# One prompt of a hybrid decoder layer with expert retrieval: all tokens in one stream, or two token streams with the second one's work placed between the expert slots

## The reference

```
h  = rmsnorm(x) @ w_in                       # columns split among four mixers
x += rmsnorm_g(mixers(h)) @ w_out            # RWKV-7, FoX attention, gated unit, dilated attention
x += cross_attend(rmsnorm(x), memory)        # 4 heads over 256 memory tokens: ca_wq, ca_wk, ca_wv, ca_wo
x += peer(rmsnorm(x))                        # expert retrieval
y  = rmsnorm(x)

def peer(x):                                 # 8 heads, 128 x 128 experts, 16 kept per head
    q = x @ peer_wq
    s = q . peer_keys                        # two halves of 128 keys per head
    e, score = the 16 best sums of both halves
    act = gelu(x . u_tab[e])                 # u_tab, v_tab: 16384 rows of 1024
    return sum(softmax(score) * act * v_tab[e])
```

## Time and profile before

| | |
|---|---|
| median of 3 runs | 1295.68 us (1295.6 to 1297.0) |
| the profiled execution | 1299.01 us, span of the trace 1297.2 us |
| mean granted clock of PE | 0.948 |
| PE, DVE, ACT, POOL busy | 1100.2, 658.9, 446.5, 380.4 us |
| first fetch of expert rows issued | 542.99 us |
| moved by all DMA queues | 387.99 MB |

### The profile page before, as it was taken

One profiled execution on the slowest core, in us unless ns is written; L12 is line 12 of the kernel. 1 busy time (PEld: TensorE's weight loads), 2 busy tenths in 40 slices (PEclk: granted clock), 3 DMA queues, 4 the chain that ended last, 5 costly groups with the idle time before them and its releaser, 6 DMA issues.

```text
span 1297.2 us, 12851 instructions
## 1 busy us (share of the span) xinstructions
PE 1100.2 (85%) x4406; PEld 604.8 (47%) x4406; DVE 658.9 (51%) x1685; ACT 446.5 (34%) x1249; POOL 380.4 (29%) x382
## 2 busy tenths in 40 slices
PE   5999999796888997989999987788777877877776
PEld 4777877564566765644444432232222322322211
DVE  2361222455311222456576666767666666667554
ACT  3232210333202212144443444434544344444343
POOL 0410012550000000124444455344443443434430
PEclk9999996897988998989999999999999999999989
DMA  9431131842164863489999999999999999999995
GB/s 306 131 99 33 33 118 58 285 150 78 45 244 153 353 242 98 141 329 416 387 428 415 401 410 427 427 427 426 426 426 427 427 426 427 426 427 427 426 427 213
DMA packets 96642, 387.99 MB, mean 299 GB/s; under 512 B 8320, under 2 KB 53312, under 8 KB 57152
## 3 DMA queue, kind: packets, MB, share of 16 engines
q0 software_dynamic: 43520, 306.24, 56.9%
q1 hardware_dynamic: 50752, 78.83, 17.5%
q10 hardware_dynamic: 2304, 2.10, 0.5%
HBM read 381.19 MB, written 5.42 MB: 298 GB/s over the span
## 4 chain that ended last, share of the span: by engine, by line
PE 53%; DMA 29%; ACT 9%; DVE 5%; POOL 2%; issue 2%; ACTq 0%; SPq 0%; POOLq 0%; DVEq 0%
DMA near<-peer_uv,idx 19%; PE ps L1106 15%; PE ps L606 14%; PE ps L614 9%; DMA far<-peer_uv,idx 8%; PE ps L714 1%; ACT L1389 1%; ACT L1400 1%; ACT dg L1409 1%; DVE near L1953 1%; PE ps L1088 1%; ACT wv L1404 1%; PE ps L985 1%; PE ps L610 1%; PE ps L1026 1%
## 5 line engine op out<-in xcount | busy, mean ns | idle before, releaser
L1106 PE MATMUL ps<-near,dg 128*128 128x512 f32 (+1 forms) x852 | 419.2, 622 | 80.2 <-ACT dg L1409 80.2
L2043 POOL DMA_INDIRECT near<-peer_uv,idx x213 | 232.6, 1092 | 404.5 <-PE ps L1106 286.0
L1953 DVE CUSTOM_DVE_ANT_0 near<-near,XN 128x1024 f32<-128x1024 f32 x192 | 235.3, 1225 | 154.3 <-DMA near<-peer_uv,idx 153.9
L1106 PEld LDWEIGHTS ps<-near,dg 128*128 128x128 f32 (+1 forms) x852 | 149.9, 187 | 313.3 <-ACT dg L1409 179.6
L1106 PE MATMUL ps<-far,dg 128*128 128x512 f32 (+1 forms) x300 | 148.7, 625 | 44.3 <-ACT dg L1409 44.3
L606 PE MATMUL ps<-xT,W 128*128 128x288 f32 x672 | 182.8, 416 | 1.3 <-DVE xT L1452 0.9
L1400 ACT ACTIVATE gl<-act 128x1 f32<-128x1 f32 x288 | 57.9, 201 | 326.0 <-DVE act L1953 325.7
L606 PEld LDWEIGHTS ps<-xT,W 128*128 128x128 f32 x672 | 129.5, 195 | 64.1 <-issue 34.6
L1409 ACT ACTIVATE dg<-const,wv 128x128 f32<-128x128 f32 (+1 forms) x288 | 113.0, 393 | 19.3 <-PE ps L1106 10.3
L1106 PEld LDWEIGHTS ps<-far,dg 128*128 128x128 f32 (+1 forms) x300 | 48.8, 179 | 142.9 <-ACT dg L1409 98.0
L2043 POOL DMA_INDIRECT far<-peer_uv,idx x75 | 78.7, 1049 | 109.8 <-PE ps L1106 101.7
(11 more groups left out here) (393 smaller groups left out, 1131.3 us busy)
## 6 DMA issues: line engine op xcount, KB each, us to landing
W<-w_in SPq DMA_DIRECT2D x11, 1024.0 KB, 5.5
MR<-mk_s SPq DMA_DIRECT2D x8, 1024.0 KB, 14.0
MR<-mv_s SPq DMA_DIRECT2D x8, 1024.0 KB, 10.6
W<-peer_wq SPq DMA_DIRECT2D x8, 1024.0 KB, 5.5
W<-ca_wk SPq DMA_DIRECT2D x4, 1024.0 KB, 5.7
W<-ca_wv SPq DMA_DIRECT2D x4, 1024.0 KB, 5.6
W<-w_out SPq DMA_DIRECT2D x4, 1024.0 KB, 6.6
W<-ca_wq SPq DMA_DIRECT2D x4, 1024.0 KB, 5.3
```

Of the source, the lines that this page charges most:

```text
L1106: ins = mm(PS[0:m, 2 + 2 * t + half, :], dg[:, n % DGS, 0:m], row(n)[:, D + half * 512:D + (half + 1) * 512], start=False, stop=False, ski ...
L1953: V.tensor_tensor_reduce(out=u, in0=u, in1=x, scale=1.0, scalar=0.0, op0=ALU.mult, op1=ALU.add, accum_out=M["act"][:, par, k:k + 1]).then_ ...
L2043: G.indirect_dma_start(row(n), None, io["peer_uv"], bass.IndirectOffsetOnAxis(ap=M["idx3"][:, it % 3, k:k + 1], axis=0))\
```

## The change

The tokens are split in two streams. Stream A has the 32 sample tokens and prompt rows 0 to 127 (160 columns), stream B prompt rows 128 to 255 (128 columns). The list `FIRST` takes A through all stages up to the key scores of heads 0 to 3 and the first selection; the fetches begin there. The list `THEN` holds the rest of A's scores and then all stages of B. It has 90 cuts, and 58 pairs of slots (`EARLY`) are spread over them evenly by `pairs_at`; the other 86 pairs follow behind the list. All of SP, PE, ACT and DVE follow the same two lists, so that a pair stands at the same cut on each. The weights of `w_in`, `w_out`, `ca_wq`, `ca_wo` and `peer_wq` are loaded twice, 72 blocks in all (32 of them for B); B's blocks use two of the three places, the third becomes a ring place (`w2`). The ring has five places, six from slot 10 and thirteen from slot 124.

A slot is now a group of 32 tokens, four heads, one rank: nine groups of 32 slots, 288 as before, 1 MB each. `dg` is 128x32, and PE combines a pair by four products of 32x512 in the four column groups of one bank (L1386). Behind a group ACT copies the bank out (`stash`; the first five go to HBM). `fin_load`, `fin_sum`, `fin_square`, `fin_scale` and `fin_store` put the groups together at set pairs. The token rows for the dots are loaded per group (`load_xr`, four broadcast copies); keys, memory keys and values and norm gains are loaded again for B, and the normed rows and the residual go through HBM. The waits of PE in a pair are for `act_dg` of the pair's second slot.

```diff
+BLOCKS = W_IN + MEMORY + TAIL + W_IN + TAIL
...
+        s = b % RING if b < SECOND else (b - SECOND) % 2
...
-NEAR, FAR = 8, 5
-WIDE = 6 * TOPK
...
+GROUPS = [0, 0, 0, 0, 2, 1, 1, 1, 1]
+NG = len(GROUPS)
+PER = 32
...
+NEAR, FAR = 5, 7
+WIDE = 124
...
-        + [("rounds", it) for it in range(NIT)] + [("finish", 2)])
...
+    THEN = (
+        [("lin", P_A + 4 + i) for i in range(4)] + [("score", ("A", 1)), ("first", 1), ("norm_b", None)]
+        + [("lin", IN_B + i) for i in range(4)]
+        + [("rw_pre", "B"), ("rw_kk", "B"), ("lin", IN_B + 4), ("rw_vec", "B"), ("rw_tile", 1), ("rw_scan", "B"),
+           ("rw_out", "B")]
+        + [("lin", IN_B + i) for i in range(5, 12)] + [("lf", "B")]
+        + [("attn", (1, s)) for s in range(11)]
+        + [("sgu", "B"), ("gnorm", ("B", (0, 2))), ("gnorm", ("B", (1, 3)))]
+        + [("lin", OUT_B + i) for i in range(4)] + [("norm", (0, "B"))] + [("lin", Q_B + i) for i in range(4)]
+        + [("cross", (1, s)) for s in range(7)]
+        + [("lin", O_B + i) for i in range(4)] + [("norm", (1, "B"))]
+        + [("lin", P_B + i) for i in range(4)] + [("score", ("B", 0))]
+        + [("lin", P_B + 4 + i) for i in range(4)] + [("score", ("B", 1))])
...
+    EARLY = 58
...
+        return range(c * EARLY // NCUTS, (c + 1) * EARLY // NCUTS)
...
+            for _ in range(n + 1):
+                for p in pairs_at(c):
+                    pair(p)
+                c += 1
+        assert c == NCUTS
+        for p in range(EARLY, PAIRS):
+            pair(p)
...
+            pe.wait_ge(*at("act_dg", n + 1))
...
-                    ins = mm(PS[0:m, 2 + 2 * t + half, :], dg[:, n % DGS, 0:m], row(n)[:, D + half * 512:D + (half + 1) * 512],
-                             start=False, stop=False, skip_group_check=True)
...
+            for x in (n, n + 1):
...
+                    rows = slice(64 * half + 32 * (x % 2), 64 * half + 32 * (x % 2) + 32)
+                    ins = mm(PS[rows, ACC, :], dg[:, x % DGS, :], row(x)[:, D + half * 512:D + (half + 1) * 512],
+                             start=x % PER < 2, stop=x % PER >= PER - 2, skip_group_check=True)
...
-                A(dg[:, n % DGS, 0:m], ident if t < 2 else cst("groupsum"), ACT.Copy, scale=M["wv"][:, par, col_k])\
...
+                A(dg[:, n % DGS, :], cst("groupsum"), ACT.Copy, scale=M["wv"][:, par, col_k]).then_inc(*inc("act_dg", n))
```

More of the change, by code:

```diff
@@ L136, in constants @@
     cols["groupsum"] = (r % TS == np.arange(TS)[None]) * 1.0
+    late = ("s_ab", "s_a", "batch", "lf_new_l", "lf_new_r", "sb_bias", "sd_bias")
+    cols = {k: cols[k] for k in [k for k in cols if k not in late] + list(late)}
     where, at = {}, 0
@@ L384, in program @@
     rT, kT, vT = hT[:, 0:2, :], hT[:, 2:4, :], hT[:, 4:6, :]
[L388 to L394, removed]
-        + [("rounds", it) for it in range(NIT)] + [("finish", 2)])
     X1, XN, gr, hX, QX, MK, MV, MR, SCx, PTx, SSx, PTy, softx = (
         M[k] for k in ("X1", "XN", "gr", "hX", "QX", "MK", "MV", "MR", "SCx", "PTx", "SSx", "PTy", "softx"))
[L398 to L425, removed]
+    keys, SA, dg, XR, FS, X1f, gF = (M[k] for k in ("keys", "SA", "dg", "XR", "FS", "X1f", "gF"))
     SC, PT, LFU, lf, soft = (M[k] for k in ("SC", "PT", "LFU", "lf", "soft"))
@@ new lines, in pair, with residual, add_group @@
+        def pair(p):
+            slot_pair()
+        def residual(t, name, count):
+            m = TILES[t][1]
+            pe.wait_ge(S.sem(name), 16 * count)
+            for half in range(2):
+                mm(PS[0:m, FIN_BANK[t] + half, :], ident[0:m, 0:m], X1f[0:m, SLOT[t], half * 512:(half + 1) * 512],
+                   start=True, stop=False, skip_group_check=True)
+        def add_group(t, j, place):
+            for half in range(2):
+                ins = mm(PS[32 * j:32 * j + 32, FIN_BANK[t] + half, :], cst("groupsum")[64 * half:64 * half + 64, :],
+                         FS[64 * half:64 * half + 64, place, :], start=False, stop=True, skip_group_check=True)
+            return ins
@@ L1951, in rounds, with pair @@
+        later = [iter(())]
+        def pair(p):
+            for n in (2 * p, 2 * p + 1):
+                it, k = divmod(n, TOPK)
+                g, par = n // PER, it % 2
+                if k == 0 and it:
+                    for _ in later[0]:
+                        pass
+                    later[0] = topk(it + 2) if it + 2 < NIT else iter(())
+                if n % PER == 0:
+                    dve.wait_ge(S.sem(f"xr{g % 2}_in"), 64 * (g // 2 + 1))
                 dve.wait_ge(S.sem(f"row{PLACE[n]}_in"), LANDINGS[n])
@@ L1971, in _ @@
             "rw_scan": rw_scan, "rw_sample": rw_sample, "rw_out": rw_out, "lf": log_forget, "attn": attn,
             "sgu": sgu, "sattn": sattn, "gnorm": gnorm, "norm": norm, "cross": cross, "scross_k": scross_k,
[L1973 to L1974 removed]
+            "scross_v": scross_v, "first": first, "fin_scale": fin_scale, "end": lambda: fin_scale(1)},
+            lambda label: None, pair)
     @block.gpsimd
```

1950 lines of the change are left out of this document (1143 added, 807 removed).

## The result

The changed kernel takes 1523.9 us (median of four, 1513.0 to 1534.0) against 1295.64 of the kernel before: a ratio of 1.177, 95% interval 1.167 to 1.187. The sign was forecast, the size was not: 1405 with a range to 1500. The profiled execution took 1518.75 us, its span is 1516.6.

The account below looks back on a forecast made before the run. First part bound by PE and waits between engines, second by bytes at 427 GB/s. 444 + 260 + 183 + 35 + 30 + 35 = 987, plus 408 + 13 + 10 = 1418, adjusted to 1405 us; range 1240 to 1500.

Parts of the forecast that it names:

- Part 2: Stream B by itself, its stages repeated at 128 columns without memory and sample work: 260 us, bounds 245 to 290.
- Part 5: Behind B: 166 slots at 2.456 are 408 us, other transfers 13, the end 10.
- (a): Rival: pairs in B hide behind other work, bytes stay the limit; 1227 us, range 1215 to 1293, chance 0.20.
- (b): Rival: pairs cost as forecast, but tables, clock and weights little; 1320 to 1340 us, slower, chance 0.12.
- (c): Rival: B's weight blocks land late behind fetches, 32 blocks add 200 us; 1580, beyond 1500 at chance 0.11.
- Part 1: Stream A with 160 columns starts fetches earlier: first fetch at 402 us instead of 543, B begins at 444.
- Part 3: 54 pairs within B: 21 behind weight blocks at 2.95 us, 33 elsewhere at 3.7, sum 183, bounds 48 to 217.
- Part 4: What mixing pairs into B adds: table loads 35 us, lower clock 30, waits for weights 35.

Follow-up runs that it names:

- all pairs in one place: Changed kernel with all 58 early pairs in one cut between the rest of stream A and B's first block, B without slots: 1516.7 us.
- three places: Changed kernel with three places instead of two for B's weights, and a ring of five instead of six until slot 124: 1484.2 us.
- pairs behind blocks: Changed kernel with B's 54 pairs only at cuts that follow a weight block, none at the other cuts: 1432.3 us.
- One pair later: Changed kernel with PE combining each pair at the place of the next pair, all else unchanged: 1406.5 us.

## Why the prediction was wrong

By its own parts, predicted and measured, in us:

| | predicted | measured | from |
|---|---|---|---|
| first fetch | 402 | 412 | the changed kernel |
| B begins | 444 | 454 | the changed kernel |
| B by itself (Part 2) | 260 (245 to 290) | 300 | all pairs in one place |
| 54 pairs and what they bring (Parts 3 and 4) | 183 + 35 + 30 + 35 = 283 | 600 - 300 = 300 | both |
| behind B (Part 5) | 408 + 13 + 10 = 431 | 462 | the changed kernel |
| sum | 1418 | 1516 | |

The mechanism was right: earlier fetches, a chain that stands in PE's stream, and the bytes behind it. Rivals (a) and (b) are out, the latter by 180 us. Of the 200 of (c) the run with three places found 40. The step that failed first of all is the price of a pair between units: 3.7 with an overlap that did not come, where the place above shows 5.65. Three other terms were too small as well, and so was the sum by the 10 that I took off for waits covering one another.

*Part 1* was late by 10, within its bounds of 385 to 415.

*Part 2* was 40 too small and 10 beyond its bound. In the run with all pairs in one place, read by stages, the products with weight blocks (and the two key scores) take 174 us where I counted 121; all else takes 126 where I counted 139. Of the 53 too many, 30.5 are PE's waits for blocks, with no pair in B; the longest:

```profile
PE ps L850 <- DMA W<-w_in: 12.0, 3, 6.7
PE ps L858 <- DMA W<-w_out: 8.5, 1, 8.5
```

My own figures had this. With two places a load goes out only when PE is done with the block that lay there, so two blocks take a landing and a block, 5.3 + 3.55 = 8.85, and not 7.1; over 32 blocks that is 28. That "at 5.3 nothing is late" needs the pairs between the blocks, and Part 2 is B without them.

A smaller part is the clock. I scaled the stages of the earlier trace rows by columns and tiles. But those rows hold stages in which PE's gaps were filled with products for the memory keys; B has no such filler. In the same run B's attention is at this clock, without any pair in it:

```profile
880.00:913.00 33.00, 27.74 (x80) 15.71 (x80) 14.75 (x49) 13.13 (x32) 0.00 (x0) 0.54 0.20 62
```

33 us at 0.54, where half of the 50 at 0.91 was expected. I had named that loss in Part 4's 30 for the clock, but sized it for B and the pairs together.

*Part 3.* The price between units was wrong in its choice: 3.7, between 4.7 for a serial chain and 2.7. In attention it is 5.65 (above), which is the serial chain with PE's part at the lower clock. The overlap that I allowed for is not there, because the dots stand behind the unit on DVE, and the unit's last step on DVE waits for PE. With the 4.7 of my upper bound, 33 pairs would have added another 33 us. PE's waits for `dg` were 210 us where I had named 100 to 150. With the 4.1 per pair of the run with pairs behind blocks, an estimate for the 33 others is (300 - 21 x 4.1)/33 = 6.5 each, table loads and clock included, where I had 3.7 + 1.2 = 4.9. These 1.6, some 53 us over 33 pairs, are what the pairs cost (300) above 183 + 35 + 30 = 248, my sum for them without the term for weights.

*Part 4*, term by term: table loads 35, measured 26. Weights 35: PE waits 29 for them in B, but 30.5 in B by itself, so the pairs added nothing to it; the number fits by luck, since I had put it down to landings behind fetches. Clock 30 (bounds 0 to 75): the zero products gave back 64, in B's own products and the pairs together. The first slot's 3.78 had shown the price at that level; I took it for an event at a stage's start. Here the 54 pairs keep PE busy for 91.7 us, 1.70 each, between the 1.06 and the 1.93 of the two levels, so most of them ran at the lower one.

The terms don't simply add. One pair later takes 117 off and three places 40; both together take 132. One later and pairs behind blocks take 117 and 92, and together 81.

*Part 5* was 31 too small. Behind B a slot does not take the 2.456 of the earlier trace rows. The DMA queues of 300 us, 1100 to 1400, in the changed kernel (all, the fetches, SP's loads), and the fetches of 900 to 1200 in the kernel before:

```profile
DMA packets 18480, 125.26 MB, mean 418 GB/s; under 512 B 2203, under 2 KB 2203, under 8 KB 3803
...
q0 software_dynamic: 16497, 120.13, 96.5%
q1 hardware_dynamic: 1825, 4.72, 4.5%
```

```profile
q0 software_dynamic: 17482, 127.30, 100.6%
```

120.13 MB are 114.6 slots in 300 us, 2.62 us each, against 121.4 and 2.47 before. From 1054 to the end the fetch queue moved 178.27 MB, 170 slots and not 166, since two slots beyond the 116 had landed by then and not six. 170 times 2.62 are 445 where I had 408 and 13 for the other transfers, 421: that is 24 of the missing 31. The end took 14 instead of 10: the last dot begins at 1502.4. The rate itself is lower with the other transfers (418 against 427). Why the mixed traffic costs 2% of the rate, no run here tells apart.

What would have had to hold for the change to win: B must end by 1297 - 462 = 835, so with B by itself at 300 and its start at 454 the 54 pairs may cost 81, 1.5 each. The cheapest way found costs (466 - 300)/54 = 3.1. What these 3.1 consist of, no run tells apart, and one pair later together with the zero products was not run.

## What to carry to other kernels

Work laid into gaps of another stream must not bring its own wait into an engine that the stream needs: count the whole chain of engines as the price, unless the consumer stands at least one step behind the producer in each engine's order (3.3 instead of 5.6 us per pair here). Before filling gaps, measure the stream without the filler (here all pairs in one place): if the time is the same, the mixing hides nothing, whatever the profile's gaps suggest. Price the stream without the filler by its own ring, too: with two places, two blocks take a landing and a block. And a stage that loses its filler is to be priced at the lower clock, not by scaling the old stage's time (attention in B: 33 us, not 25).

## What the runs showed of the hardware that was not expected

Zero products in PE's waits made the kernel 64 us faster (1459.8 against 1523.9) by holding the granted clock at 0.91 instead of 0.70. In the changed kernel PE stood 210 of 600 us before its pairs, and the clock over that stretch was 0.70; with all pairs in one place B alone, without these waits, was at 0.80.

With six places for fetches DMA was busy at a share of 1.00 and moved 399 GB/s, with thirteen in the kernel before 427 at 1.01. The share of busy time alone thus didn't tell what was moved. Transfers other than fetches were 2% of the bytes there; behind B, with thirteen places, they were 4%, and the rate was 418. That the number of places makes the difference was not tested by itself.
